# RWKV-7 recurrence: the chunk inverse's lower levels on 32 x 32 diagonal blocks, its last level as one block

## What is computed

```
def step(S, inp):
    r_t, w_t, k_t, v_t, kk_t, b_t = inp
    sa = jnp.einsum('bhvk,bhk->bhv', S, -kk_t)
    S = S * w_t[:, :, None, :] + sa[..., None] * b_t[:, :, None, :] + v_t[..., None] * k_t[:, :, None, :]
    return S, jnp.einsum('bhvk,bhk->bhv', S, r_t)
```

## Time and profile before

| what | value |
|---|---|
| median of 3 runs | 2952.13 us (2950.14 to 2952.67) |
| the profiled execution's own time | 2951.57 us |
| its span, first to last instruction | 2949.8 us |
| mean granted TensorE clock | 0.983 of full |
| TensorE busy | 2809.1 us, 37104 matmuls |
| VectorE, ScalarE, GpSimd busy | 1329.7, 1135.4, 106.7 us |
| the recurrence loop | about 910 to 1482 us of the span |
| queue that brings instructions (q8) | 294 packets, 4.82 MB |

### The profile page before, as it was taken

One profiled execution on the slowest core, in us unless ns is written; L12 is line 12 of the kernel. 1 busy time (PEld: TensorE's weight loads), 2 busy tenths in 40 slices (PEclk: granted clock), 3 DMA queues, 4 the chain that ended last, 5 costly groups with the idle time before them and its releaser, 6 DMA issues.

```text
span 2949.8 us, 81345 instructions
## 1 busy us (share of the span) xinstructions
PE 2809.1 (95%) x37104; PEld 2642.2 (90%) x37104; DVE 1329.7 (45%) x2185; ACT 1135.4 (38%) x1567; POOL 106.7 (4%) x91
## 2 busy tenths in 40 slices
PE   5999999999999999999889899999999999999995
PEld 4899999999997888887789889999999999998995
DVE  4434323313326787777632354344433444334223
ACT  5444323324414555555432343332333333334221
POOL 0000000000000010000000000000000000000000
PEclk8999999999999999999999999999999999999998
DMA  3233333334211111112132242222222232222322
GB/s 122 87 102 109 112 115 115 109 109 142 100 64 52 53 52 52 52 52 76 30 128 86 84 137 84 84 96 88 88 73 95 79 105 78 83 95 70 114 88 97
DMA packets 77318, 262.27 MB, mean 89 GB/s; under 512 B 15664, under 2 KB 21552, under 8 KB 56496
## 3 DMA queue, kind: packets, MB, share of 16 engines
q1 hardware_dynamic: 67760, 239.23, 24.0%
q10 hardware_dynamic: 9216, 17.83, 1.6%
HBM read 216.06 MB, written 40.97 MB: 87 GB/s over the span
## 4 chain that ended last, share of the span: by engine, by line
PE 47%; DVE 1%; ACT 1%; issue 1%; ACTq 0%; DVEq 0%
PE t_pair L129 40%; PE t_lev L1498 1%; PE t_tok L1561 1%; PE t_lev L1572 1%; PE t_tok L1454 1%; PE t_tok L1579 0%; PE t_lev L1549 0%; PE t_tok L1539 0%; DVE keep_o L1837 0%; PE t_lev L1551 0%; PE t_lev L1511 0%; PE t_tok L1522 0%; PE t_tok L1531 0%; PE t_lev L1506 0%; PE t_tok L1533 0%
## 5 line engine op out<-in xcount | busy, mean ns | idle before, releaser
L129 PE MATMUL t_pair<-t_x_hi,keep_w_hi 128*128 128x272 f32 x3072 | 674.6, 301 | 26.3 <-DVE t_x_lo L1842 16.9
L129 PE MATMUL t_pair<-t_x_lo,keep_w_hi 128*128 128x272 f32 x3072 | 637.6, 289 | 0.0
L129 PE MATMUL t_pair<-t_x_hi,keep_w_lo 128*128 128x272 f32 x3072 | 637.3, 289 | 0.0
L129 PEld LDWEIGHTS t_pair<-t_x_hi,keep_w_hi 128*128 128x128 f32 x3072 | 480.8, 189 | 57.7 <-issue 26.0
L129 PEld LDWEIGHTS t_pair<-t_x_lo,keep_w_hi 128*128 128x128 f32 x3072 | 486.4, 189 | 0.0
L129 PEld LDWEIGHTS t_pair<-t_x_hi,keep_w_lo 128*128 128x128 f32 x3072 | 483.1, 189 | 0.0
L129 PE MATMUL w_pair<-a_x_hi,keep_w_hi 128*128 128x272 f32 x2048 | 437.2, 294 | 23.8 <-ACT a_x_hi L848 19.1
L129 PE MATMUL w_pair<-a_x_hi,keep_w_lo 128*128 128x272 f32 x2048 | 426.2, 290 | 0.0
L129 PE MATMUL w_pair<-a_x_lo,keep_w_hi 128*128 128x272 f32 x2048 | 426.0, 290 | 0.0
L968 DVE TENSOR_TENSOR keep_w_lo<-keep_raw,keep_w_hi 128x2048 fp32r<-128x2048 f32 x64 | 146.7, 2293 | 517.5 <-ACT keep_w_hi L750 517.5
L129 PEld LDWEIGHTS w_pair<-a_x_hi,keep_w_hi 128*128 128x128 f32 x2048 | 327.2, 190 | 31.2 <-issue 21.0
(11 more groups left out here) (326 smaller groups left out, 3653.1 us busy)
## 6 DMA issues: line engine op xcount, KB each, us to landing
keep_raw<-in_w_in SPq DMA_DIRECT2D x64, 1024.0 KB, 4.9
keep_raw<-in_hgrn_in SPq DMA_DIRECT2D x64, 1024.0 KB, 4.9
keep_raw<-in_rwkv_wo SPq DMA_DIRECT2D x16, 1024.0 KB, 4.9
keep_raw<-in_hgrn_wo SPq DMA_DIRECT2D x16, 1024.0 KB, 4.9
t_Ss<-in_hgrn_s SPq DMA_DIRECT2D x16, 512.0 KB, 4.4
out_hgrn_s<-t_Sd SPq DMA_DIRECT2D x16, 512.0 KB, 6.6
a_nxt<-in_x SPq DMA_DIRECT2D x4, 1088.0 KB, 9.4
scr_r<-a_stage ACTq DMA_DIRECT2D x16, 272.0 KB, 2.1
```

The costliest lines, as they stand in the source:

```text
L129: mm = pe.matmul(out[:, a, 0:TH], w, x[:, kt, a * TH:(a + 1) * TH], start=(kt == 0 and n == 0), stop=(kt == KT - 1 and n == 2))
```

## The change

Levels 1 to 4 now work on the 32 x 32 blocks on the diagonal alone, four for each chunk (two heads, two halves of 64 tokens). They are kept side by side in tiles dT, dTi and X that are half as wide (128 x 256 in place of 128 x 512). `diagonal`, new on ScalarE, copies the result into TiT in four copies of 32 partitions; the rest of TiT is zeroed once by GpSimd. Level 5 is one 32 x 32 block per head and chunk, and its mask and its addition become plain copies of two groups of 32 partitions. `each(...)`, `cut(...)` and `stacked(...)` are as in the functions above. The masks in the constant table shrink from 64 to 32 columns.

```diff
-        lev = [tables[f"lev{m}"] for m in RWKV_LEVELS]
+        lev = [tables[f"lev{m}"] for m in RWKV_LEVELS[:5]]
         NL = len(RWKV_LEVELS) - 1
+        NUP = NL + 1
+        BK = C // 2
...
-        MT, Mak, Mrb, TiT, Ti, X = (early.sb(n, [P, SEQ]) for n in ("MT", "Mak", "Mrb", "TiT", "Ti", "X"))
+        MT, Mak, Mrb, TiT = (early.sb(n, [P, SEQ]) for n in ("MT", "Mak", "Mrb", "TiT"))
+        dT, dTi, X = (early.sb(n, [P, SEQ // 2]) for n in ("dT", "dTi", "X"))
...
+        def grp(n):
+            return slice(BK * n, BK * n + BK)
+
+        def own_block(t, c, n):
+            return t[grp(n), C * c + BK * (n % 2):C * c + BK * (n % 2) + BK]
+
+        def blk(t, c, n):
+            return t[grp(n), BK * c:BK * c + BK]
...
             def level_x(j, l):
...
                 for c in range(NCH):
-                    mm = stacked(cut(level_ps(j), c), cut(MT, c), cut(Ti, c))
+                    if l < NL:
+                        for n in range(4):
+                            mm = pe.matmul(blk(out, c, n), own_block(MT, c, n), blk(dTi, c, n), start=True, stop=True)
+                    else:
+                        for n in (0, 2):
+                            mm = pe.matmul(blk(out, c, n + 1), MT[grp(n), C * c + BK:C * c + C], blk(dTi, c, n),
+                                           start=True, stop=True)
...
             def level_yt(j, l):
-                pe.wait_ge(s.X, NL * j + l)
+                pe.wait_ge(s.X, NUP * j + l + (l == NL))
+                out = level_ps(j)
                 for c in range(NCH):
-                    mm = stacked(cut(level_ps(j), c), cut(X, c), cut(TiT, c))
+                    for n in range(4) if l < NL else (1, 3):
+                        mm = pe.matmul(blk(out, c, n if l < NL else n - 1), blk(X, c, n), blk(dT, c, n),
+                                       start=True, stop=True)
...
             def first_right(i):
                 pe.wait_ge(s.mrb, i + 1)
-                pe.wait_ge(s.tit, NL * (i + 1))
+                pe.wait_ge(s.tit, NUP * (i + 1))
+                pe.wait_ge(s.diag, 4 * (i + 1))
...
-                act.copy(by_chunk(TiT), each(k.eye)).then_inc(s.eyed, 1)
+                act.copy(by_block(dT), each_block(k.eye32)).then_inc(s.eyed, 1)
...
+            def diagonal(j):
+                if j == 0:
+                    act.wait_ge(s.zeroed, 4)
+                act.wait_ge(s.tit, NUP * j + NL - 1)
+                for n in range(4):
+                    cols = slice(BK * (n % 2), BK * (n % 2) + BK)
+                    act.copy(by_chunk(TiT)[grp(n), :, cols], by_block(dT)[grp(n)]).then_inc(s.diag, 1)
...
                 if back:
                     act.wait_ge(s.lnv, i + 1)
                     act.activation(rs[:, :], rs[:, :], ACT.Exp, scale=-0.5).then_inc(s.rs, 1)
+                if front:
+                    diagonal(j)
...
-            for t in (at_b, bds, kds):
+            for t in (at_b, bds, kds, TiT):
...
             def mask_x(j, l):
                 dve.wait_ge(s.x_mm, NL * j + l)
-                dve.tensor_tensor(by_chunk(X), by_chunk(level_ps(j)), each(lev[l]), ALU.mult).then_inc(s.X, 1)
+                if l < NL:
+                    dve.tensor_tensor(by_block(X), by_block(level_ps(j)), each_block(lev[l]), ALU.mult).then_inc(s.X, 1)
+                else:
+                    for n in (1, 3):
+                        dve.tensor_copy(X[grp(n), :], level_ps(j)[grp(n), 0:SEQ // 2]).then_inc(s.X, 1)
 
             def add_tit(j, l):
                 dve.wait_ge(s.yt_mm, NL * j + l)
-                dve.tensor_tensor(TiT[:, :], level_ps(j)[:, :], TiT[:, :], ALU.add).then_inc(s.tit, 1)
+                if l < NL:
+                    dve.tensor_tensor(dT[:, :], level_ps(j)[:, 0:SEQ // 2], dT[:, :], ALU.add).then_inc(s.tit, 1)
+                else:
+                    for n in (0, 2):
+                        dve.tensor_copy(by_chunk(TiT)[grp(n), :, BK:C], by_block(level_ps(j))[grp(n)]).then_inc(s.tit, 1)
...
-                dve.transpose(Ti[:, :], TiT[:, :]).then_inc(s.ti, 1)
+                dve.transpose(dTi[:, :], dT[:, :]).then_inc(s.ti, 1)
...
-                dve.copy_predicated(by_chunk(TiT), each(lev[0]).bitcast(mybir.dt.int32), by_chunk(c1_ps)).then_inc(s.tit0, 1)
+                for n in range(4):
+                    cols = slice(BK * (n % 2), BK * (n % 2) + BK)
+                    dve.copy_predicated(by_block(dT)[grp(n)], each_block(lev[0]).bitcast(mybir.dt.int32)[grp(n)],
+                                        by_chunk(c1_ps)[grp(n), :, cols]).then_inc(s.tit0, 1)
```

More of the change, by code:

```diff
@@ L154, in rwkv @@
         sq, rstd = stage, mix[0]
-        names = ["reset", "bones", "center", "strict", "incl", "eye", "s_mask", "seq", "lev1"]
-        names += [f"lev{m}" for m in RWKV_LEVELS[1:]]
+        names = ["reset", "bones", "center", "strict", "incl", "eye", "s_mask", "seq", "eye32"]
+        names += [f"lev{m}" for m in RWKV_LEVELS[:5]]
         col0, col1 = keep.col[names[0]][0], sum(keep.col[names[-1]])
@@ L201, in rwkv @@
                    "r0ta_mm r0 ta u0_mm u0 g_mm g wh_mm rhoe_mm rhoe chain_mm state y_mm y_ev eyed "
-                   "strict_mm MT tit0 ti x_mm X yt_mm tit mak "
+                   "strict_mm MT tit0 ti x_mm X yt_mm tit diag mak "
                    "incl_mm mrb mrk bk_mm btok ktok av_mm atok vtok "
@@ L241, in by_chunk, with by_block, each_block @@
             return t[:, c0 * C:SEQ].rearrange("p (c t) -> p c t", t=C)
+        def grp(n):
[4 more added lines that the diff above has]
+            return t[grp(n), BK * c:BK * c + BK]
+        def by_block(t):
+            return t[:, 0:BK * NCH].rearrange("p (c t) -> p c t", t=BK)
+        def each_block(mask):
+            return mask[:, :].unsqueeze(1).broadcast_to([P, NCH, BK])
         def each(mask, c0=0):
@@ L477, in b_and_k_by_token @@
                 pe.wait_ge(s.MT, j + 1)
-                pe.wait_ge(s.tit0, j + 1)
+                pe.wait_ge(s.tit0, 4 * (j + 1))
                 pe.wait_ge(s.mak, j + 1)
@@ L834, in first_pair @@
                     key_root(1)
+                elif n == 62:
+                    diagonal(0)
                 elif n == NT - 1:
@@ L1111, in first_pair @@
                     bonus_out(0)
-                    dve.wait_ge(s.zeroed, 3)
+                    dve.wait_ge(s.zeroed, 4)
                     sample_inputs(0)
@@ L2068, in constants @@
     t["seq"] = twice((tt[:, None] >= 0) & (tt[:, None] // DS == np.arange(NB)[None, :]))
-    t["lev1"] = twice(level_t(one, 1, 1))
-    for m in RWKV_LEVELS[1:]:
-        t[f"lev{m}"] = twice(level_t(one, 1, m).T)
-    pad = lambda a: np.concatenate([a, np.zeros((P - a.shape[0], a.shape[1]))])
     i32 = np.arange(32)
     four = lambda a: np.concatenate([a] * 4) * 1.0
+    t["eye32"] = four(np.eye(32))
+    t["lev1"] = four(level_t(i32, 1, 1))
+    for m in RWKV_LEVELS[1:5]:
+        t[f"lev{m}"] = four(level_t(i32, 1, m).T)
+    pad = lambda a: np.concatenate([a, np.zeros((P - a.shape[0], a.shape[1]))])
     t["h_diag"] = four(np.eye(32))
```

4 lines of the change are left out of this document (2 added, 2 removed).

## The result

The change makes the kernel slower: 3054.66 us median of four runs (3049.65 to 3064.22) against 2951.39, a ratio of 1.0353 (95% interval 1.0331 to 1.0375), +103 us. The forecast was 3010 us, slower, with 2963 to 3045 as its range. The direction was right, and so was the mechanism that the forecast priced highest, the fetch of instructions; the time lies 10 us above the range.

The account below looks back on a forecast made before the run. TensorE's list was taken to stand just under the instruction fetch bound. A step: +4.6 - 0.4 = +4.2 us, 15 steps +63, dense phase -3.5, together +59 on 2951.6: 3010 us, range 2963 to 3045.

Parts of the forecast that it names:

- What bounds the kernel: Loop: TensorE's own list, just under an instruction fetch bound of 67 instructions per us while it starves.
- The cycle read from two stalls: TensorE's instruction fetch: a block of 256 instructions every 3.84 or 3.83 us, from two "issue" stalls in the profile.
- Rival A: Fetch is no limit at this length, only execution counts, and the kernel gets faster: 2899 us; chance 0.14.
- The level stretch: First level stage to `rank_w`: 512 added instructions make it fetch-bound, 22.1 us against 17.5, +4.6 us a step.
- The dense phase: Pair 0's ten stages lie under it, with few instructions per us, so the shorter stages gain there: -3.5 us.
- The first Ti: Ahead of the first level stage: one predicated copy becomes four, 0.4 us net a step, covered by the level stretch's growth.
- The end of the step: `rank_w` to the next `first_right`: 5.8 us along ScalarE's chain against 6.2, a gain of 0.4 us a step.
- The start of the step: `first_right` to `bonus`: the forecast's sum had no term for it.
- Rival C: Fetch binds and the granted clock falls to half in part of the level stretch: 3035 us; chance 0.12.

Follow-up runs that it names:

- three_bursts: Kernel before plus three bursts of 512 products on constant data in the dense phase (64 x 64 and 32 x 32 tiles); 3036.22 us, +84.
- half_products: Changed kernel with two of four 32 x 32 products left out in levels 1 to 4, their addition multiplied by zero; 2964.74 us against 2952.19 for the kernel before.
- added_products: Kernel before with 16 extra 32 x 32 products ahead of each stage of levels 1 to 4, pairs 1 to 15, adding 512 instructions a step; 3048.33 us, +98.
- one_pred: Changed kernel with only one of the four predicated copies ahead of the first level stage kept; 3043.55 us in one run.
- level5_alone: Kernel before with only level 5 changed: one 32 x 32 product per head and chunk, mask and addition two copies each; 2967.37 us, ratio 1.0057.
- one_diag: Changed kernel with only one of the four ScalarE copies of `diagonal` kept; 3058.26 us.
- wide_columns: Changed kernel with 64 in place of 32 moving columns in the products of levels 1 to 4, same instruction count; 3058.46 us, ratio to before 1.0363.
- half_wide: half_products with 64 in place of 32 moving columns in levels 1 to 4; 3033.95 us.
- block_diagonal: Half-wide tiles with the kernel before's 64 x 64 products (32 moving columns), no added instructions, `diagonal`'s copies as one GpSimd operation; 2987.54 us, ratio 1.0124 to before.

## Why the prediction was right and wrong

**What bounds the kernel: right, and the point of the case.** The cycle read from two stalls came back as 3.8 us in the bursts. Rival A (2899 us, 0.14) is out by three_bursts, half_products and added_products together.

**The level stretch: right.** +4.6 us forecast, +5.13 measured; 22.1 against 22.7 us. The stages execute as computed: 64 matmuls in 0.75 us (1148.90 to 1149.65) against 0.73. The groups of the other tile shape before and behind them overlap these 64 by 0.08 and 0.06 us in the trace (ends of matmuls are modelled), so no idle time shows at these two changes; what a change costs, no run isolates, and the 0.8 us that I took off for 20 of them stay unproven.

**The dense phase: right.** -3.5 us forecast, the loop starts 3.7 earlier.

**The first Ti: failed.** "That costs 0.4 us net unless something slower covers it", then "covered": it cost 0.99. Four predicated copies last 1.84 us, 0.46 each with no overlap between them, where I had 0.4 each with overlap. And nothing covered it: the path from bonus to level 1 is VectorE's (with one copy in place of four it is 1.04 us shorter, one_pred).

```profile
1137.85 1.84 DVE L1112 COPY_PREDICATED b_dT<-b_table,w_pair 32x256 f32<-32x256 int32 x4
```

**The end of the step: failed, and by sign.** "This end of the step gains 0.4" became a loss of 0.83. "Level 5's mask and addition become two copies each, about even" was the mistake: they cost 0.75 us there (level5_alone). The copies of `diagonal` take 0.42 each, not 0.3; ScalarE is ready at about the same time as VectorE (one_diag). I had followed ScalarE's chain and not VectorE's list beside it. In the change itself, whose transpose there takes 0.45 us in place of 0.71, the end is 6.61 us at full clock, +0.38. The rest, to 7.06 on average, goes with half clock: it stands in the five ends named above, up to 8.75 us in a step.

**The start of the step: failed, as it was left out.** The sum had no term for it, and it grew by 0.68. At full clock it is +0.34 (4.59); level5_alone has as much, +0.39, with neither the added instructions nor a lower clock (0.99 over its loop), so the last level's form probably brings it. The other 0.34 goes with half clock. How it would get there, no run shows.

These three cost 2.5 us a step (0.99 + 0.83 + 0.68), 37 us in 15 steps, where the forecast had a gain of 6 us: a miss of 43 us, of which some 12 go with half clock. The level stretch adds 15 x 0.5 = 8, together 51, where 3010 and 3055 are 45 apart: the steps are those of the profiled execution, which is 8 us or so further from the kernel before (111) than the medians are (103). The range was built from the fetch cycle and the clock, and held no bound for these three. That the level stretch came out within 0.5 us is partly luck: the forecast had it at full clock, and it had 5 us at half clock.

**Rival C, the clock: in part right.** It did fall (0.89 over the loop), and I gave it 3035 us, for the level stretch alone. What can be read, some 12 us, stands at the two ends of a step. added_products has a loss of the same size without it, so it isn't the main cause; more than halving it in wide_columns brought the median nothing, in a kernel that executes longer, so its share can't be fixed closer. Where the fetch does not bind, its price is plain: 8 us in a step of half_wide.

## What to carry to other kernels

Count a change in instructions of the busiest queue over the stretch where they fall, before counting its arithmetic: here a block of 256 takes 3.8 us even where it executes in less, and with the smaller tiles a stage needs twice the instructions. A stall for "issue" in the middle of a group of ready products is the sign, and packets of the instruction queue at the same spacing bear it out. And an operation split by partitions costs its whole length again each time; look at which engine's list ends a stretch before crediting another engine with a saving there. And read the granted clock of a variant before taking its time as the worth of the part that it leaves out.

## What the runs showed of the hardware that was not expected

- An instruction on 32 partitions and 256 elements takes VectorE 0.44 to 0.46 us, as one on 128 partitions does (0.43 in the earlier trace rows), and four in a row do not overlap (1.84 us).
- Two VectorE operations took 1.52 and 1.36 us beside GpSimd operations, against 0.74 and 0.78 where GpSimd was idle (block_diagonal).
- TensorE's granted clock was 0.66 in a burst that was busy almost without a break (64 x 64 on two tiles, 32 moving columns), 1.00 in one that was idle 42% of the time, and it was at half longest, 151 us of 14 steps, in half_wide, a kernel with more work per product.
